# Packed weights, a 512-column output projection and stream keys by channel in a hybrid encoder step

## The chip, the cores and the metric

The kernel runs on one core of one Trainium2 chip. The metric is the device time of one launch, in microseconds. Work on the host before and after the launch (laying out inputs, reshaping outputs) is outside of it.

## What is computed

One layer of a streaming encoder, for 1024 prompt tokens and 8 streams of 16 new tokens, each stream with 512 past keys. All data is fp32.

```
h = RMSNorm(x) * g_pre;  z = h @ w_in                 # 2048 -> 7760 columns: q k v ga qi ki wi bg cg hc gb
iscore = sum_h relu(qi_h . ki) * wi_h                 # 16 index heads of 64 channels
sel = top_k(iscore, 256)  (132 for a stream)          # keys of later 64-frame chunks excluded
attn = softmax(q . k[sel]) @ v[sel]                   # 8 heads, 2 key/value heads, 128 channels
conv = bg * conv3(cg * hc)                            # causal, depthwise
y = x + RMSNorm(concat(attn*silu(ga), conv*silu(gb)) @ w_out) * g_post
```

Also returned: the new k, v and ki of every token, and the last two rows of cg*hc.

## The kernel before

Activations lie transposed on chip (`act_hi`, `act_lo`: 128 channels by 16 channel blocks by tokens). Each fp32 product is made as three fp32r products: high times high, high times low, low times high. ScalarE rounds a weight block to `w_hi` (`split_high`, line 1085), GpSimd makes the rest `w_lo` (line 813), VectorE makes the low parts of other operands (`low`, line 1338).

The work is a list of 154 tiles, each cut into 8 slots. Group A is 512 prompt tokens and the 128 stream tokens, group B the other 512 prompt tokens. Tiles 0 to 60 are the input projection of A (`gemm`, line 884: 96 matmuls a tile, 320 columns each), 61 to 121 that of B (48 of 512 columns), 122 to 137 the output projection of A, 138 to 153 that of B (`out_gemm`, line 914). There the stationary operand is a 128-token block of activations and the moving one 256 columns of `w_out`: 8 column groups ("pairs" of tiles), 5 token blocks in A and 4 in B. When a pair of tiles is done, VectorE multiplies all of its blocks by g_post (`product_out`, line 1475) and ScalarE sums their squares (`product_squares`, line 1176); the next pair goes on in the banks that are free. A's products go through `o_stage` to memory (`z_og`), B's stay in `o_nat`.

A planner (`timetable`) puts the attention's steps into slots by widths (`W`) that stand for their time. Every engine walks the same slots: the projection's part first, then the slot's steps. Each engine is a queue in order, SyncE (SP) too, which issues all DMAs. So a step waits for what lies ahead of it on its own engine. The steps that matter here:

- QS, IKS, HS, SEL (tiles 32 to 38, index scores of the streams). QS loads the index queries of all streams. IKS(b) loads 512 past index keys of stream b by token, transposes them on TensorE (4 transposes) and copies them. HS(b, 0 or 1) are two plain fp32 matmuls of 8 heads by 264 keys each (line 967), relu and weighting; SEL sums over heads (line 976).
- S, NRM, PT, ZZ (softmax of the prompt): scores (line 933), exponent (1235), normalising (1553), transposes (841), `pt_hi`/`pt_lo`, value product (984), gate (1594). Those of A and of the streams lie in tiles 62 to 76, those of B in tiles 109 to 131.
- KS, SS, PS, VS (softmax of the streams). KS(b) loads past keys by token, transposes them (8 transposes) and copies them to `kts`.
- RMS and FIN: the last norm and the residual sum (line 1633), 5 blocks of A beside the output projection of B, 4 blocks of B after its end.

`turn` (tiles kiwi, k, v) transposes new keys and values back to rows for the outputs. A weight half-tile of 512 KB comes by one DMA in rows of 512 bytes (1 KB for `w_out`), three buffers deep.

## Time and profile before

| | |
|---|---|
| runs | 2347.27, 2348.95, 2344.57 us; median 2347.27 |
| profiled execution | 2350.01 us; span from first to last instruction 2348.2 us |
| TensorE matmul busy | 2264.2 us, 96% of the span; granted clock 0.99 on average |
| VectorE / ScalarE / GpSimd busy | 992.8 (42%) / 718.2 (31%) / 757.9 us (32%) |
| chain that ended last | TensorE 84%, of it line 884 57% and line 914 16% of the span; VectorE 9% |
| DMA | 276.85 MB in 404152 packets, 382753 of them under 2 KB |

The busy share of TensorE is a union of instructions whose ends are modelled. To see what a matmul costs, take a run of matmuls with nothing between them from the chain of waits and divide its length by their number. Where the chain leaves TensorE, TensorE was waiting for the piece named.

### The profile page before, as it was taken

How to read it: one execution, taken by the hardware profiler on the slowest of the kernel's cores; microseconds unless marked ns; L12 is line 12 of the kernel's file. 1: busy time of each engine (PE TensorE's matmuls, PEld its weight loads, DVE VectorE, ACT ScalarE, POOL GpSimd, SP SyncE). 2: the span in 40 equal slices, each digit the busy share in tenths (PEclk: the TensorE clock that was granted, in tenths of full speed). 3: DMA queues.
4: the chain of work that ended last, by engine and by line, in shares of the span. 5: the costliest groups of instructions: out<-in, count | busy, mean ns of one | idle time of the engine just before them, and what ended most of it. 6: DMA issues, size and time to landing. Idle time of an engine off the chain costs nothing.

```text
span 2348.2 us, 33612 instructions
## 1 busy us (share of the span) xinstructions
PE 2264.2 (96%) x13997; PEld 2084.1 (89%) x13997; DVE 992.8 (42%) x1702; ACT 718.2 (31%) x1089; POOL 757.9 (32%) x328
## 2 busy tenths in 40 slices
PE   5999999999999999999998999999999999999996
PEld 5999998999999999877777888887877899999996
DVE  4000006891161112355213969797885634303212
ACT  5121123312211124343333242424223633324221
POOL 4333332232233333322222434342432222233442
PEclk9999999999999999999999999999999999999998
DMA  4433342343223244454654433334342524137644
GB/s 163 118 91 104 104 110 64 88 89 84 67 78 87 78 124 137 115 149 129 174 152 123 128 104 103 98 103 110 87 123 81 192 79 126 52 108 236 244 146 169
DMA packets 404152, 276.85 MB, mean 118 GB/s; under 512 B 36065, under 2 KB 382753, under 8 KB 401953
## 3 DMA queue, kind: packets, MB, share of 16 engines
q1 hardware_dynamic: 404000, 274.71, 40.1%
q8 instruction: 111, 1.82, 0.3%
q14 instruction: 41, 0.33, 0.0%
HBM read 230.58 MB, written 44.09 MB: 117 GB/s over the span
## 4 chain that ended last, share of the span: by engine, by line
PE 84%; DVE 9%; issue 2%; ACT 2%; DMA 2%; SPq 1%; DVEq 0%; ACTq 0%
PE ps L884 57%; PE ps L914 16%; PE ps L933 4%; PE ps L841 2%; PE ps L984 2%; DVE isc L1515 2%; DVE top L1514 1%; PE ps L1056 1%; DVE act_lo L1338 1%; DVE isc L1502 1%; DVE F L1553 1%; PE ps L967 1%; DMA conv<-z_mix 1%; DVE F L1577 1%; DMA w_raw<-in_w_in 0%
## 5 line engine op out<-in xcount | busy, mean ns | idle before, releaser
L813 POOL TENSOR_TENSOR w_lo<-w_raw,w_hi 128x1024 fp32r<-128x1024 f32 x308 | 743.2, 2413 | 1538.0 <-ACT w_hi L1085 1537.9
L884 PE MATMUL ps<-act_hi,w_hi 128*128 128x320 f32 (+1 forms) x2928 | 839.9, 340 | 6.8 <-DVE act_lo L1338 4.1
L884 PE MATMUL ps<-act_hi,w_lo 128*128 128x320 f32 (+1 forms) x2928 | 831.2, 337 | 0.0
L884 PE MATMUL ps<-act_lo,w_hi 128*128 128x320 f32 (+1 forms) x2928 | 831.0, 337 | 0.0
L884 PEld LDWEIGHTS ps<-act_hi,w_hi 128*128 128x128 f32 x2928 | 512.4, 189 | 54.0 <-issue 14.2
L1085 ACT ACTIVATE w_hi<-w_raw 128x1024 fp32r<-128x1024 f32 x308 | 326.1, 1059 | 753.4 <-PE ps L884 533.1
L884 PEld LDWEIGHTS ps<-act_hi,w_lo 128*128 128x128 f32 x2928 | 512.0, 188 | 39.6
L884 PEld LDWEIGHTS ps<-act_lo,w_hi 128*128 128x128 f32 x2928 | 512.7, 189 | 35.4
L914 PE MATMUL ps<-w_hi,act_hi 128*128 128x256 f32 x1152 | 326.9, 284 | 1.6 <-ACTq L1152 1.0
L914 PE MATMUL ps<-w_hi,act_lo 128*128 128x256 f32 x1152 | 326.1, 283 | 0.0
L914 PE MATMUL ps<-w_lo,act_hi 128*128 128x256 f32 x1152 | 326.0, 283 | 0.0
L914 PEld LDWEIGHTS ps<-w_hi,act_hi 128*128 128x128 f32 x1152 | 220.8, 192 | 4.2 <-ACTq L1152 1.2
L914 PEld LDWEIGHTS ps<-w_lo,act_hi 128*128 128x128 f32 x1152 | 220.9, 192 | 1.9
L914 PEld LDWEIGHTS ps<-w_hi,act_lo 128*128 128x128 f32 x1152 | 221.0, 192 | 0.0
L1514 DVE MAX8 top<-isc 128x8 f32<-128x384 f32 (+6 forms) x209 | 183.9, 880 | 9.9 <-DVE cs_p L1404 0.5
L1515 DVE MATCH_REPLACE8 isc<-top,isc 128x384 f32<-128x384 f32 (+6 forms) x209 | 180.0, 861 | 0.0
L1502 DVE SCALAR_TENSOR_TENSOR isc<-ps,wi_nat,isc 128x384 f32<-128x384 f32 (+5 forms) x90 | 85.6, 951 | 59.6 <-ACT ps L1199 54.5
L841 PE MATMUL ps<-ident,F 128*128 128x128 f32 (+2 forms) x504 | 76.8, 284 | 26.9 <-DVE F L1365 11.9
L1338 DVE TENSOR_TENSOR pt_lo<-ps,pt_hi 128x512 fp32r<-128x512 f32 x72 | 49.5, 690 | 121.0 <-ACT pt_hi L1085 121.0
L1148 ACT ACTIVATE ev<-ps 128x640 f32<-128x640 f32 (+1 forms) x58 | 37.6, 648 | 203.7 <-PE ps L884 203.7
L1199 ACT ACTIVATE ps<-ps 128x384 f32<-128x384 f32 (+5 forms) x96 | 68.0, 740 | 98.6 <-PE ps L933 98.6
L1526 DVE MEMSET msk<- 128x64 uint32 (+1 forms) x2 | 0.3, 138 | 228.9 <-DMA z_mask<-msk 228.6
(147 smaller groups left out, 1522.8 us busy)
## 6 DMA issues: line engine op xcount, KB each, us to landing
w_raw<-in_w_in SPq DMA_DIRECT2D x244, 512.0 KB, 4.0
w_raw<-in_w_out SPq DMA_DIRECT2D x64, 512.0 KB, 4.2
qraw<-z_qi SPq DMA_DIRECT2D x24, 256.0 KB, 4.8
fin_x<-in_x_prompt SPq DMA_DIRECT2D x6, 1024.0 KB, 8.3
conv<-z_mix SPq DMA_DIRECT2D x16, 320.0 KB, 4.0
z_og<-ev SPq DMA_DIRECT2D x8, 640.0 KB, 4.5
fin_o<-z_og SPq DMA_DIRECT2D x5, 1024.0 KB, 5.4
out<-fin_o SPq DMA_DIRECT2D x10, 512.0 KB, 5.0
```

Source lines behind the costliest of these rows:

```text
L813: nc.gpsimd.tensor_tensor(w_lo[:, r], w_raw[:, r], w_hi[:, r].bitcast(F32), ALU.subtract).then_inc(sem_w_lo, 1)
L841: return nc.tensor.transpose(out, in_, ident[0:in_.shape[0], 0:in_.shape[0]])
L884: last = nc.tensor.matmul(ps[:, bank + x, 0:w], wt[:, r, k % 8], a[:, k, w * x:w * (x + 1)], start=(k == 0 and wt is w_hi and a is act_hi) ...
L914: last = nc.tensor.matmul(out_place(pair, i), a[:, kk, z], out_weights(wt, h)[:, k], start=(kk == 0 and part == 0 and opens), stop=(kk == ...
L933: last = nc.tensor.matmul(ps[:, bank + x, 0:c], lhs, rhs[:, c * x:c * (x + 1)], start=(i == 0), stop=(i == len(operands) - 1))
L984: last = nc.tensor.matmul(ps[:, 4, :], lhs[:, P * j:P * j + P], rhs[:, p % 2], start=(j == 0 and i == 0), stop=(j == count - 1 and i == 2))
L1085: return nc.scalar.activation(out, in_, ACT.Copy)
L1199: nc.scalar.activation(v, v, ACT.Relu, scale=(ID * IH * 1.0) ** -0.5).then_inc(sem_relu, 1)
L1338: return nc.vector.tensor_tensor(out, x, hi.bitcast(F32), ALU.subtract)
L1502: ins = nc.vector.scalar_tensor_tensor(out=like(isc), in0=v, scalar=wi, in1=like(isc), op0=ALU.mult, op1=ALU.add)
L1514: link(nc.vector.max(top8[:], isc[:, 0:w]))
L1515: link(nc.vector.match_replace(isc[:, 0:w], top8[:], isc[:, 0:w], NEG_TAKEN))
```

## The change

The output projection takes 512 columns of `w_out` at a time: 4 column groups of 4 tiles. A has now 4 token blocks there, B has 5 (the stream block moved from A to B). Each block has a bank of its own and is multiplied, squared and, in A, stored by itself, one slot after its last matmul; A's stores go through three staging rows (`o_stage`). B uses eight banks. The activations of B are converted from tile 134 on, behind A's last column group. The softmax steps of B beside the output projection are placed 1.2 times as wide (`so`). FIN does 4 blocks beside B and 5 after it.

The host lays out `w_in` and `w_out` so that one DMA of a half-tile reads rows of 4 KB, and hands over `cache_k` and `cache_idx_k` by channel. The transposes of IKS and KS go away. New k and ki are outputs by channel, and k is not turned any more. KS has two buffers, and starts loading only when the last PT of A is done. The index queries of the streams are loaded twice, into partitions 0 to 63 and 64 to 127; ScalarE rounds all, VectorE makes the upper half the low part, and HS multiplies this stacked operand by the high and then by the low part of the keys (loaded twice too): four fp32r matmuls of 264 columns instead of two fp32 ones.

```diff
--- before.py
+++ after.py
...
-OUTP = [("o", i, 2 * P * (i // 2)) for i in range(KT)]
-OW, PAIRS = 2 * P, KT // 2
+OUTP = [("o", i, 4 * P * (i // 4)) for i in range(KT)]
+OW, PAIRS = 4 * P, KT // 4
+COLUMNS = [t[:2] for t in PROJ["A"]]
+OT = {"A": 4, "B": 5}
+OUT_COLUMN = {"A": 0, "B": 512}
+OUT_TOKENS = {"A": 512, "B": T_ALL - 512}
+SHARE = {"A": ((0,), (1,), (2,), (3,)), "B": ((0, 1), (2,), (3,), (4,))}
...
-TURNED = ("kiwi", "k", "v")
+TURNED = ("kiwi", "v")
...
+Z_B = SLOTS * (OUT_B - 4) + 4
 def z_pieces(slot):
 
     n, s = divmod(slot, SLOTS)
     if n == PHASE_LAST[1]:
         return [(0, 2 * s), (0, 2 * s + 1)]
-    if n == PHASE_LAST[2]:
-        return [(1, 2 * s), (1, 2 * s + 1)] if s < 4 else [(1, 4 + s)]
-    return [(1, 12 + s)] if n == PHASE_LAST[2] + 1 and s < 4 else []
+    c, late = divmod(slot - Z_B, 4)
+    return [(1, 2 * c), (1, 2 * c + 1)] if 0 <= c < KT // 2 and not late else []
+def z_loads(slot):
+    n, s = divmod(slot, SLOTS)
+    if n == PHASE_LAST[1]:
+        return [(0, k) for k in range(KT) if s == max(0, (k - 4) // 2)]
+    c, late = divmod(slot + 7 - Z_B, 4)
+    return [(1, 2 * c), (1, 2 * c + 1)] if 0 <= c < KT // 2 and not late else []
+def ended(slot):
+    n, s = divmod(slot - 1, SLOTS)
+    if not 0 <= n < NT or TILES[n][1] != "o" or TILES[n][2] % 4 != 3 or s < 4:
+        return []
+    return [(n, i) for i in SHARE[TILES[n][0]][s - 4]]
...
-    place([(step, 2) for step in second] + softmax_b[cut:], 2 * NP + 1.7, OUT_B - 1)
-    place([(("RMS", "A"), 3)] + [(("FIN", i), 16) for i in range(5)], OUT_B + 1, OUT_B + 14)
-    side[TAIL] = [("RMS", "B")] + [("FIN", i) for i in range(5, 9)]
+    place([(step, 2) for step in second] + wider(softmax_b[cut:], W["so"]), 2 * NP + 1.7, OUT_B - 1)
+    place([(("RMS", "A"), 3)] + [(("FIN", i), 16) for i in range(4)], OUT_B + 1, OUT_B + 14)
+    side[TAIL] = [("RMS", "B")] + [("FIN", i) for i in range(4, 9)]
...
-    if kind in ("KS", "QI") and n > 0:
+    if kind == "QI" and n > 0:
         return same[n - 1]
+    if kind == "KS":
+        return [s for s in ORDER if s[0] == "SS"][n - 2] if n > 1 else [s for s in before_it if s[0] == "PT"][-1]
...
+        o_stage = [ev[:, 0, 0:OW], ev[:, 1, 0:OW], conv[:, 2560:3072]]
...
+        qs_raw = F[:, 0:2048].rearrange("p (b h q) -> p b h q", b=NB, h=IH)
+        qs_v = qv[:].rearrange("p (b h q) -> p b h q", b=NB, h=IH)
+        ik_raw = F[:, 2048:2048 + 2 * KEYS_S].rearrange("p (u x) -> p u x", u=2)
+        r_s = F[:, 3104:3104 + KEYS_S]
+        ik_hi = [keys_hi[:, 0:KEYS_S], q_hi[:].rearrange("p u t -> p (u t)")[:, 0:KEYS_S]]
+        ik_lo = [keys_lo[:, 0:KEYS_S], q_lo[:].rearrange("p u t -> p (u t)")[:, 0:KEYS_S]]
+        kts = F[:, 0:4 * KEYS_S].rearrange("p (u k x) -> p u k x", u=2, k=2)
...
+            return 4 * pair + i if pair < PAIRS else 4 * PAIRS + 5 * (pair - PAIRS) + i
 
         def out_place(pair, i):
-            return ps[:, bank_use(pair, i) % 4, OW * (i % 2):OW * (i % 2 + 1)]
+            use = bank_use(pair, i)
+            return ps[:, use % 4 if pair < PAIRS else (use - 4 * PAIRS) % 8, 0:OW]
...
+                    _, kind, index, _ = TILES[h // 2]
+                    src = w_in[COLUMNS.index((kind, index)), h % 2] if kind != "o" else \
+                        w_out[index // 4, 2 * (index % 4) + h % 2]
+                    sp.dma_start(w_raw[:, h % RING].rearrange("p k e -> p (k e)"), src
+                                 ).then_inc(sem_w_ld[h % RING], 16)
...
+            def store_product(n, i):
+                c, use = TILES[n][3], bank_use(TILES[n][2] // 4, i)
+                sp.wait_ge(sem_o_cp, use + 1)
+                sp.dma_start(z_og[P * i:P * (i + 1), c:c + OW], o_stage[use % 3]).then_inc(sem_og_out[use % 3], 16)
...
+                    for r in range(2):
+                        for b in range(NB):
+                            c = 512 + NS * b
+                            sp.dma_start(qs_raw[ID * r:ID * r + ID, b], z_qi[:, c:c + NS].rearrange("(h d) q -> d h q", d=ID)
+                                         ).then_inc(sem_qs_ld, 16)
...
-                    sp.dma_start(ik_new, z_kiwi[0:ID, 512:T_A]).then_inc(sem_qs_ld, 16)
+                                         ).then_inc(sem_wi_ld, 16)
                 elif kind == "IKS":
                     b = step[1]
+                    spilled("A", "kiwi", 0)
                     sp.wait_ge(sem_x_read, 5)
-                    sp.wait_ge(sem_iks_tr, max(b - 1, 0))
-                    sp.dma_start(iknat[:, b % 2], cache_idx_k[0, b].rearrange("(t p) d -> p t d", p=P)
-                                 ).then_inc(sem_iks_ld[b % 2], 16)
+                    sp.wait_ge(sem_iks_lo, max(b - 1, 0))
+                    for r in range(2):
+                        part = ik_raw[ID * r:ID * r + ID, b % 2]
+                        sp.dma_start(part[:, 0:PAST], cache_idx_k[b]).then_inc(sem_iks_ld[b % 2], 16)
+                        sp.dma_start(part[:, PAST:KEYS_S], z_kiwi[0:ID, 512 + NS * b:512 + NS * (b + 1)]
+                                     ).then_inc(sem_iks_ld[b % 2], 16)
...
-                    sp.wait_ge(sem_ks_tr, b)
-                    sp.dma_start(knat, cache_k[0, b].rearrange("(t p) k d -> p t (k d)", p=P)
+                    sp.wait_ge(sem_pt_pe, PT_A)
+                    sp.wait_ge(sem_ss_pe, max(b - 1, 0))
+                    sp.dma_start(kts[:, b % 2, :, 0:PAST], cache_k[b]).then_inc(sem_ksk_ld[b % 2], 16)
+                    c = 512 + NS * b
+                    sp.dma_start(kts[:, b % 2, :, PAST:KEYS_S], z_k[:, c:c + NS].rearrange("(k d) t -> d k t", d=P)
                                  ).then_inc(sem_ksk_ld[b % 2], 16)
...
+                pair, c, h = index // 4 + PAIRS * (group == "B"), 2 * (index % 4) + s // 4, 2 * n + s // 4
                 if s % 4 == 0:
                     pe.wait_ge(sem_w_lo, h + 1)
-                units = [(k, i) for j in range(0, tiles, 2) for k in range(4) for i in range(j, min(j + 2, tiles))]
-                for x, (k, i) in enumerate(units[tiles * (s % 4):tiles * (s % 4 + 1)]):
-                    kk = 4 * quarter + k
+                for i in SHARE[group][s % 4]:
                     use = bank_use(pair, i)
-                    if kk == 0 and i % 2 == 0:
+                    if c == 0:
                         if use < 4:
                             pe.wait_ge(sem_evac[use // 2], NP)
-                        pe.wait_ge(sem_nat_sq, max(use - 3, 0))
-                    if pair % PAIRS == 0 and i == 0:
-                        pe.wait_ge(sem_z_lo, kk + 1 + KT * (group == "B"))
-                    z = slice(P * i, P * (i + 1))
-
-                    opens, closes = i % 2 == 0, i % 2 == 1 or i == tiles - 1
-                    for part, (a, wt) in enumerate(((act_hi, w_hi), (act_hi, w_lo), (act_lo, w_hi))):
-                        last = nc.tensor.matmul(out_place(pair, i), a[:, kk, z], out_weights(wt, h)[:, k],
-                                                start=(kk == 0 and part == 0 and opens),
-                                                stop=(kk == KT - 1 and part == 2 and closes))
+                        elif pair < PAIRS:
+                            pe.wait_ge(sem_nat_sq, use - 3)
+                        else:
+                            pe.wait_ge(sem_nat_sq, max(use - 7, 4 * PAIRS))
+                            if use == 4 * PAIRS + 4:
+                                pe.wait_ge(sem_z_dve, UNITS)
+                    for k in range(2):
+                        kk, z = 2 * c + k, slice(P * i, P * (i + 1))
+                        if pair % PAIRS == 0 and i == 0:
+                            pe.wait_ge(sem_z_lo, kk + 1 + KT * (group == "B"))
+                        for part, (a, wt) in enumerate(((act_hi, w_hi), (act_hi, w_lo), (act_lo, w_hi))):
+                            last = nc.tensor.matmul(out_place(pair, i), a[:, kk, z], out_weights(wt, h)[:, k],
+                                                    start=(kk == 0 and part == 0), stop=(kk == KT - 1 and part == 2))
+                    if c == KT // 2 - 1 and i < OT[group] - 1:
+                        last.then_inc(sem_o_pe, 1)
...
-                elif kind == "IKS":
-                    b = step[1]
-                    pe.wait_ge(sem_iks_ld[b % 2], 16 * (b // 2 + 1))
-                    pe.wait_ge(sem_isum, HEADS_A)
-                    pe.wait_ge(sem_hs_r, 2 * b)
-                    for t in range(4):
-                        last = transpose(ps[0:ID, 4, P * t:P * t + P], iknat[:, b % 2, t])
-                    last.then_inc(sem_iks_tr, 1)
                 elif kind == "HS":
                     _, b, j = step
-                    pe.wait_ge(sem_iks_cp, b + 1)
-                    pe.wait_ge(sem_qs_ld, 16 * 25)
+                    pe.wait_ge(sem_iks_lo, b + 1)
+                    pe.wait_ge(sem_qs_lo, 1)
+                    pe.wait_ge(sem_isum, HEADS_A)
                     pe.wait_ge(sem_hs_r, n)
+                    lhs = qs_v[:, b, 8 * j:8 * j + 8].rearrange("p h q -> p (h q)")
                     for x in range(2):
-                        lhs = qs_v[:, b, 8 * j:8 * j + 8].rearrange("p h q -> p (h q)")
-                        last = nc.tensor.matmul(ps[:, 4 + x, 0:HALF_S], lhs, ikt[:, HALF_S * x:HALF_S * (x + 1)],
-                                                start=True, stop=True)
+                        cut = slice(HALF_S * x, HALF_S * (x + 1))
+                        for i, rhs in enumerate((ik_hi[b % 2], ik_lo[b % 2])):
+                            last = nc.tensor.matmul(ps[:, 4 + x, 0:HALF_S], lhs, rhs[:, cut], start=(i == 0), stop=(i == 1))
                     last.then_inc(sem_hs_pe, 1)
...
-                    pe.wait_ge(sem_ksk_ld[b % 2], 16 * (b // 2 + 1))
-                    pe.wait_ge(sem_z_dve, UNITS_A)
-                    pe.wait_ge(sem_ps_cp, max(b - 1, 0))
-                    for kv in range(2):
-                        for t in range(4):
-                            last = transpose(ps[:, 4 + kv, P * t:P * t + P], knat[:, t, P * kv:P * kv + P])
-                    last.then_inc(sem_ks_tr, 1)
                 elif kind == "SS":
                     b = step[1]
-                    pe.wait_ge(sem_ks_cp, b + 1)
-                    pe.wait_ge(sem_qqs_ld, 16 * (NB + 2))
+                    pe.wait_ge(sem_ksk_ld[b % 2], 32 * (b // 2 + 1))
+                    pe.wait_ge(sem_qqs_ld, 16 * (NB + 1))
+                    pe.wait_ge(sem_z_dve, UNITS_A)
...
+            def product_squares(n, i):
 
                 group, _, index, _ = TILES[n]
+                pair = index // 4 + PAIRS * (group == "B")
+                use = bank_use(pair, i)
+                act.wait_ge(sem_nat_sq, max(use - 1, 0))
...
+                act.wait_ge(sem_o_cp, use + 1)
+                nc.scalar.activation(o_junk[use % 2], out_place(pair, i), ACT.Square,
+                                     accum_out=o_ssq[:, i, index // 4:index // 4 + 1]).then_inc(sem_nat_sq, 1)
...
+                elif kind == "QS":
+                    act.wait_ge(sem_qs_ld, 16 * 2 * NB)
+                    act.wait_ge(sem_head_pe, HEADS_A)
+                    copy(qv[:], F[:, 0:2048]).then_inc(sem_qs_hi, 1)
                 elif kind == "IKS":
                     b = step[1]
-                    act.wait_ge(sem_iks_tr, b + 1)
-                    act.wait_ge(sem_hs_pe, 2 * b)
-                    if b == 0:
-                        act.wait_ge(sem_qs_ld, 16 * 25)
-                    copy(ikt[:, PAST:KEYS_S], ik_new[:, NS * b:NS * (b + 1)])
-                    copy(ikt[:, 0:PAST], ps[0:ID, 4, :]).then_inc(sem_iks_cp, 1)
+                    act.wait_ge(sem_iks_ld[b % 2], 64 * (b // 2 + 1))
+                    act.wait_ge(sem_head_pe, HEADS_A)
+                    act.wait_ge(sem_hs_pe, 2 * max(b - 1, 0))
+                    copy(ik_hi[b % 2], ik_raw[:, b % 2]).then_inc(sem_iks_hi, 1)
...
+            def product_out(n, i):
 
                 group, _, index, c = TILES[n]
+                pair = index // 4 + PAIRS * (group == "B")
+                use = bank_use(pair, i)
+                if i == OT[group] - 1:
+                    dve.wait_ge(sem_gemm, 2 * n + 2)
+                else:
+                    dve.wait_ge(sem_o_pe, use - pair + 1)
...
                 if group == "A":
-                    dve.wait_ge(sem_og_out, 16 * pair)
-                if pair == PAIRS:
+                    dve.wait_ge(sem_og_out[use % 3], 16 * (use // 3))
+                if use == 4 * PAIRS:
                     dve.wait_ge(sem_z_out, 16 * UNITS)
+                out = o_stage[use % 3] if group == "A" else o_nat[:, i, c:c + OW]
+                nc.vector.tensor_tensor(out, out_place(pair, i), gbc[:, c:c + OW], ALU.mult).then_inc(sem_o_cp, 1)
...
+                elif kind == "QS":
+                    dve.wait_ge(sem_qs_hi, 1)
+                    low(qv[64:128, :], F[64:128, 0:2048], qv[64:128, :]).then_inc(sem_qs_lo, 1)
+                elif kind == "IKS":
+                    b = step[1]
+                    dve.wait_ge(sem_iks_hi, b + 1)
+                    low(ik_lo[b % 2], ik_raw[:, b % 2], ik_hi[b % 2]).then_inc(sem_iks_lo, 1)
...
+        if name == "w_in":
+            a = np.stack([a[0, :, col:col + P].reshape(2, 8, P, P).transpose(0, 2, 1, 3).reshape(2, P, 8 * P)
+                          for _, _, col in PROJ["A"]])
+        if name == "w_out":
+            a = a[0].reshape(8, 2, P, PAIRS, OW).transpose(3, 0, 2, 1, 4).reshape(PAIRS, 8, P, 2 * OW)
...
+        if name == "cache_k":
+            a = a[0].transpose(0, 3, 2, 1)
+        if name == "cache_idx_k":
+            a = a[0].transpose(0, 2, 1)
```

## Rows read from the trace of the kernel before

**Rows 1.** Page, section 1: busy us, share, instructions.
```profile
PE 2264.2 (96%) x13997; PEld 2084.1 (89%) x13997; DVE 992.8 (42%) x1702; ACT 718.2 (31%) x1089; POOL 757.9 (32%) x328
```

**Rows 2.** Groups by line and shape, TensorE: count, busy us, mean ns, idle before.
```profile
L884 PE MATMUL ps<-act_hi,w_hi 128*128 128x512 f32 x976 | 386.9, 396 | 2.4 <-DVEq L1428 1.5 <-DVEq L1406 0.6 <-PE ps L841 0.3
L914 PE MATMUL ps<-w_hi,act_hi 128*128 128x256 f32 x1152 | 326.9, 284 | 1.6 <-ACTq L1152 1.0 <-ACT nat L1176 0.4
```

**Rows 3.** Chain of waits, whole span: start us, us, what.
```profile
120.56 246.40 PE ps L884 x1680
...
549.47 3.72 PE ps L884 x24
554.27 3.72 PE ps L884 x24
...
1509.09 91.13 PE ps L884 x402
...
2055.77 75.61 PE ps L914 x630
```

**Rows 4.** The 64 records of line 967 (HS): duration ns, first and last start.
```profile
L967 PE MATMUL ps<-F x64: 382/383/488, 533.9 to 645.9; 64*128 64x264 f32 x64
```

**Rows 5.** Chain, 0 to 75 us: one `turn` of five transposes.
```profile
61.50 0.55 PE ps L841 x5
```

**Rows 6.** Chain, 543 to 552 us: one IKS.
```profile
544.43 0.44 PE ps L841 x4
```

**Rows 7.** Chain, 1153 to 1172 us: one KS.
```profile
1157.28 0.87 PE ps L841 x8
```

**Rows 8.** Timeline, end: VectorE, then SP's DMA issues: start us, us.
```profile
2330.59 1.42 DVE L1475 TENSOR_TENSOR o_nat<-ps,gbc 128x256 f32<-128x256 f32 x4 [21.62 <-PE ps L914]
...
2334.74 4.88 DVE L1633 SCALAR_TENSOR_TENSOR o_nat<-o_nat,stat,fin_x 128x1024 f32<-128x1024 f32 x4
...
2336.06 8.70 SPq L725 DMA_DIRECT2D out<-o_nat  x8
```

**Rows 9.** Groups by line and shape, VectorE and ScalarE.
```profile
L1594 DVE TENSOR_TENSOR zat<-ps,sga 128x512 f32<-128x512 f32 x16 | 11.0, 690 | 23.1 <-PE ps L984 23.1
L1085 ACT ACTIVATE pt_hi<-ps 128x512 fp32r<-128x512 f32 x72 | 43.0, 597 | 115.5 <-PE ps L841 115.5
L1577 DVE CUSTOM_DVE_ANT_0 F<-ps,msk 128x1024 f32<-128x1024 f32 x8 | 9.7, 1218 | 8.0 <-PE ps L933 8.0
L1235 ACT ACTIVATE F<-F,stat 128x1024 f32<-128x1024 f32 x8 | 9.2, 1151 | 17.2 <-DVE stat L1581 17.2
L1338 DVE TENSOR_TENSOR qv<-qraw,qv 64x1024 fp32r<-64x1024 f32 x12 | 23.5, 1961 | 17.0 <-ACT qv L1085 16.3
L1338 DVE TENSOR_TENSOR q_lo<-qraw,q_hi 128x512 fp32r<-128x512 f32 x16 | 16.9, 1054 | 3.5 <-ACT q_hi L1085 3.3
L1085 ACT ACTIVATE qv<-qraw 128x1024 fp32r<-128x1024 f32 x12 | 12.6, 1048 | 0.0
```

**Rows 10.** TensorE timeline, 2147.5 to 2149.6 us: first matmul that waited in B.
```profile
2148.85 0.39 PE L914 MATMUL ps<-w_hi,act_hi 128*128 128x256 f32 x1 [0.22 <-ACT nat L1176]
```

**Rows 11.** Stretch of A's output projection with softmax: busy of each engine, clock, DMA.
```profile
1853.00:2059.00 206.00, 204.08 (x1548) 196.81 (x1547) 82.47 (x168) 79.51 (x149) 47.90 (x20) 1.00 0.32 99
```

**Rows 12.** VectorE timeline at tile 32, its last work before HS.
```profile
528.08 0.82 DVE L1427 TENSOR_TENSOR conv<-ps,conv 128x640 f32<-128x640 f32 x1
```

**Rows 13.** SP timeline, the loads of QS and the weight load behind them.
```profile
490.12 7.49 SPq L613 DMA_DIRECT2D F<-z_qi  x8
...
507.43 0.59 SPq L520 DMA_DIRECT2D w_raw<-in_w_in  x1
```

**Rows 14.** DMA issues: count, KB each, median us from issue to landing.
```profile
w_raw<-in_w_in SPq DMA_DIRECT2D x244, 512.0 KB, 4.0
...
out<-o_nat SPq DMA_DIRECT2D x8, 512.0 KB, 3.0
F<-z_qi SPq DMA_DIRECT2D x8, 64.0 KB, 3.6
```

221 lines of the change are left out of this document (89 added, 132 removed).

## Prediction

> **What bounds the kernel now.** First the page: TensorE is busy 2264.2 of 2348.2 us and no other engine half of that [rows 1]; the reader sees that only TensorE can set the time. Then the runs of matmuls in the chain of waits, for the busy time does not say what a matmul costs [rows 3]: 246.40 us / 1680 = 146.7 ns for 320 columns, 91.13 / 402 = 226.7 ns for 512, 75.61 / 630 = 120.0 ns for 256. The three lie on one line: 192 columns more cost 80.0 ns, so 2.4 columns a nanosecond (the upper of the clock's two levels; the stretch of rows 11 shows a granted clock of 1.00) and 13.3 ns that each matmul costs whatever its width. The 154 tiles at these prices are some 1938 us; the rest of the span is attention work on TensorE and waits. So what counts is how many TensorE instructions go, and where TensorE would wait anew.
>
> **The change part by part.**
>
> Output projection. Before, 3 x 1152 = 3456 matmuls of 256 columns [rows 2] at 120.0 ns: 414.9 us (rounded to the 120.1 of all of them: 415.1). After: 4 column groups x 9 token blocks x 16 channel blocks x 3 = 1728 of 512 columns at 226.7: 391.7. Term: -23.3 us. The columns are the same; what goes is 1728 times the fixed 13.3. The Trainium skill, "TensorE: Matmul & The Clock Gate", section "Back-to-back issue gap", gives N / 2.4 + 2.5 ns for a warm matmul; by that the term would be only 1728 x 2.5 = 4.3 us. The rows show 13.3 at all three widths, in a stream where each matmul has a weight load of its own, so the measurement decides.
>
> HS in fp32r. From one run of 24 matmuls to the next it is 554.27 - 549.47 = 4.80 us with one HS between; 24 x 0.1467 = 3.52, so one HS costs TensorE 1.28 us [rows 3]. It is four records of 264 columns (64 in 16 steps) [rows 4]. After: four fp32r matmuls at 264 / 2.4 + 13.3 = 123.3 ns, 0.49 us. 16 x 0.79 = -12.6 us. Bounds: if a part of the 1.28 is lost at the border between kinds and stays, 0.4 of it does, +6; if nothing else, 0.
>
> Transposes that go: IKS 8 x 0.44 = 3.5 us [rows 6]; KS 8 x 0.87 = 7.0 us [rows 7]; k tiles, two of A at 0.55 [rows 5] and two of B with four transposes, 0.44 [rows 6], 2.0 us. Together -12.5. They lie between projection matmuls on the engine that bounds, so all of it counts. ScalarE's copies of them and VectorE's copies of k go too; these engines have room [rows 11], so that is worth nothing by itself. KS's place in the plan stays.
>
> End. B has 5 blocks behind its last matmul instead of 4. The eight stores of four blocks follow each other at (8.70 - 0.33) / 7 = 1.20 us, the pace of the final sums (4.88 / 4) [rows 8]; two more are +2.4. Before them one product of 512 columns (0.69) and one square (0.60 and the reading of the sum, some 0.2) [rows 9] take the place of four products (1.42) [rows 8] and squares up to 2.4 us: -0.7. Term +1.7, bounds +1 and +3.5 (the stores' DMA, 3.0 us each [rows 14], may set the pace).
>
> Border from A to B. B's first matmul asks for all 16 squares of A, and the 16th belongs to the block that ended just before it. TensorE waits for the last matmul's latency beyond its turn (0.39 - 0.23), product 0.69, square 0.60 + 0.2, hand-overs 0.1: 1.8 us; before it waited 0.22 once in B [rows 10]. Term +1.6, bounds +1 and +2.5. In exchange B's first activations are converted long before.
>
> Waits in A's output projection. A bank is wanted again three slots after its last matmul: 3 x 6 x 0.2267 = 4.1 us, and softmax work of the slots besides. Product and square need 1.6, so 2.5 are spare. Ahead of the product on VectorE may stand one score step of 1024 keys (mask and maximum 1.22, small ones, the division of the head before, about 2.6 together), ahead of the square one exponent, 1.15 [rows 9]: at worst 2.6 + 1.4 - 2.5 = 1.5 us each, for the 8 reuses (two ends of column groups) that lie beside softmax: 12 us. At best the 206.00 - 204.08 = 1.9 us of idle TensorE in this stretch before [rows 11] go too. Softmax itself has slots that are shorter (1.36 for 1.80 us), but 1.2 times as many, and VectorE is busy 82 of 206 us. I take 3 us, +1.1 net, nearest to the row, bounds -2 and +12. The three staging rows: a store of 256 KB must land within about three slots; one of 512 KB takes 3.0 [rows 14], so it is hidden. If SP comes late with it, that is in the same 12.
>
> QS and IKS. VectorE is at work until 528.9 [rows 12], then lows of 2 x 1.96 and 1.05 [rows 9]: 533.9. ScalarE's copy of the queries (2 x 1.05) lies beside VectorE's older work. The first HS was at 533.9 before [rows 4], and 0.4 us of IKS ahead of it are gone: +0.6, bounds 0 and +4. SP holds up the queue behind QS for 507.43 - 490.12 = 17.3 us; eight more loads at 7.49 / 8 make it 24.3 [rows 13]. The weight load behind them is then 7 us later; it feeds tile 32's second half, wanted at about 528, and needs 4.0 [rows 14] and two roundings (some 3.5): ready at about 522. Hidden, with 6 us to spare.
>
> KS loads start behind the last PT now, six slots (8.2 us and more) before SS(0); one of 512 KB takes 4 us: hidden. SP must wait there and issues 20 DMAs behind it, at 0.45 us each 9 us, about four slots with their softmax work; by the plan the weight load behind them is wanted eight slots later.
>
> Packed weights. No wait of the projections' matmuls is put down to a weight load [rows 2]. The load may land in 3.0 instead of 4.0 us, as the stores with 4 KB rows do [rows 14]. Three stand among the input loads before the first matmul: -0.5, bounds +0.5 and -3.
>
> Sum: -23.3 - 12.6 - 12.5 + 1.7 + 1.6 + 1.1 + 0.6 - 0.5 = -43.9 us. The profiled execution took 2350.0 (span 2348.2 and 1.8 around it), so 2306.1; the median of the runs is 2.7 below the profiled one: 2303.4, I say 2303.
>
> **The rivals.**
>
> Drains hold TensorE (12 us and more instead of 1.1 in A). For: all is in order on VectorE and ScalarE, and a bank has one owner. Against: VectorE is 60% idle there. 2303 + 11 = 2314, up to 2320.
>
> Halving the number buys nothing: the 13.3 ns goes with 256 columns and not with an instruction, 240 ns for 512. Then the first term is 0 and the time 2326. Against: line 884 shows 226.7 at 512 columns. The skill's 2.5 ns (same page and section) would come close to this in its result, at 2322.
>
> HS keeps its border cost, since SEL stays plain fp32: 2309.
>
> The other side: SP chokes on QS. 16 loads of 64-byte pieces instead of 8 fill the queues; if each blocks SP until the one before has landed (3.6 us [rows 14]), they take 58 us instead of 7.5. Beyond 13 us more than before (7 to reach the slack above, 6 of slack), the weights come late and TensorE stands: at 3.6 us a load 50 - 13 = 37 us of standing, 2340; under their own crowd, at 5 us a load, 80 - 7.5 - 13 = 59 us, 2362, slower than before. It decides from about 4.0 us a load on. Against: the eight took 0.94 each.
>
> That the change does not do what it says: the counts of matmuls would show it; I see nothing for it.
>
> **How the numbers follow.** Forecast (2296 to 2311) 0.76; drains 0.09 (2311 to 2320); HS border 0.06 (about 2309); 240 ns for 512 columns 0.03; SP 0.02, most of it beyond 2347; anything else 0.03, a quarter of it not faster. The skill's 2.5 ns has 0.01 besides. Range 2292 to 2320: below, every wait at its best bound and the opening's 3 us with some of the softmax waits of tiles 109 to 121 falling away; above, the drains' bound. About 0.2% of the time is what a measurement of this kernel can tell from none, 4.7 us: faster 0.97, same 0.01, slower 0.02.
>
> **What would show it.** Chain: runs of 512-column matmuls in the output projection at 226.7 ns each. TensorE records at the new HS line 64 of 264 columns, 0.5 us a step. About 114 transposes fewer. The output projection from its first matmul to the last some 457 us where it was 477. TensorE waits of about 1.8 us once, at the first matmul of B, and together under 5 us in A. Ten final sums, 1.2 us apart. Packets down from 404152 to 130 to 150 thousand, and nothing on TensorE moving by it. The prediction is wrong if matmuls of 512 columns cost over 230 ns, if TensorE waits more than 8 us in A's output projection, or if tiles 29 to 33 show a wait for weights.

## The result, and the profile after

| | before | after |
|---|---|---|
| runs, us | 2347.27, 2348.95, 2344.57, 2345.94 | 2312.73, 2311.65, 2310.35, 2317.49 |
| median | 2346.61 | 2312.19 |
| profiled execution (span) | 2350.01 (2348.2) | 2312.73 (2310.9) |

The ratio is 0.9857, 95% interval 0.9838 to 0.9876: 34.4 us faster, where 43.9 were forecast (about 2303 us). Between the two profiled executions the difference is 37.3 us, and these two are what the tables below take apart.

Page of the kernel after, section 1 (busy us, share, instructions), and the line of packets:

```profile
PE 2220.0 (96%) x12155; PEld 1978.3 (86%) x12155; DVE 1013.0 (44%) x1667; ACT 707.2 (31%) x994; POOL 759.8 (33%) x328
...
DMA packets 160680, 274.65 MB, mean 119 GB/s; under 512 B 42656, under 2 KB 94880, under 8 KB 158624
```

TensorE is still the only engine that can set the time, with 1842 instructions fewer than in [rows 1]: 1728 in the output projection and 114 transposes. Groups by line and shape of the kernel after, to set against [rows 2] and [rows 4] (count, busy us, mean ns, idle before):

```profile
L947 PE MATMUL ps<-w_hi,act_hi 128*128 128x512 f32 x576 | 227.0, 394 | 9.2 <-issue 4.7 <-ACTq L1173 4.5
L996 PE MATMUL ps<-q_hi,qv 128*128 128x264 f32 x16 | 4.2, 282 | 0.0
```

The first line says more than its count: 9.2 us of idle TensorE in two pieces, where [rows 2] had 1.6 in all. The chain of waits of the kernel after gives the price of a wide matmul, its timeline an HS step (start us, us, what):

```profile
2084.89 206.73 PE ps L947 x912
```
```profile
543.05 0.29 PE L996 MATMUL ps<-q_hi,qv 128*128 128x264 f32 x1
543.17 0.29 PE L996 MATMUL ps<-q_lo,qv 128*128 128x264 f32 x1
543.30 0.28 PE L996 MATMUL ps<-q_hi,qv 128*128 128x264 f32 x1
543.42 0.28 PE L996 MATMUL ps<-q_lo,qv 128*128 128x264 f32 x1
543.53 0.46 PE L916 MATMUL ps<-act_hi,w_hi 128*128 128x320 f32 x2
```

206.73 / 912 = 226.7 ns, as [rows 3] had it for the projections; an HS step is 543.53 - 543.05 = 0.48 us.

Where the 37.3 us between the two profiled executions come from, by the starts of the projection matmuls that open the tiles:

| stretch | before | after | difference |
|---|---|---|---|
| to the start of tile 32 | 521.0 | 517.3 | -3.7 |
| tiles 32 to 39, stream index | 143.8 | 128.5 | -15.3 |
| tiles 40 to 70 | 463.3 | 463.8 | +0.5 |
| tiles 71 to 76, key loads and KS | 113.2 | 107.1 | -6.1 |
| tiles 77 to 89 | 174.2 | 169.1 | -5.1 |
| tiles 90 to 121 | 437.8 | 437.0 | -0.8 |
| output projection, first matmul to last | 476.9 | 468.4 | -8.5 |
| behind the last matmul's start | 17.9 | 19.7 | +1.8 |

The forecast for the output projection was 457. Its matmuls did get shorter by 23.2 us (3456 at 120.1 against 1728 at 226.7 ns), but 14.7 us of waits and slow matmuls came in. Two places hold 12.2 us of them; the rest is spread.

**The entry (tile 122).** TensorE, then ScalarE of the kernel after; below them the granted clock of TensorE (the number behind the parenthesis) by stretch:

```profile
1831.61 0.80 PE L947 MATMUL ps<-w_hi,act_hi 128*128 128x512 f32 x1 [4.48 <-ACTq L1173]
```
```profile
1827.32 1.15 ACT L1259 ACTIVATE F<-F,stat 128x1024 f32<-128x1024 f32 x1 [2.09 <-DVE stat L1608]
...
1828.47 1.13 ACT L1106 ACTIVATE act_hi<-conv 128x512 fp32r<-128x512 f32 x2
...
1829.62 1.28 ACT L1169 ACT_TABLE_LOAD   x1
...
1830.91 0.60 ACT L1169 ACTIVATE ev<-ps 128x512 f32<-128x512 f32 x1
```
```profile
1822.00:1831.60 9.60, 5.12 (x23) 0.97 0.51 159
1831.60:1838.00 6.40, 6.39 (x22) 0.77 0.92 287
```

The third block of the first column group opens bank 2, which still holds tile 121. ScalarE empties it (1830.91) behind an exponent, two pieces of A's gated output and a table load. TensorE waits 4.65 us. Before, a bank held two half-width blocks, the same bank was wanted two blocks later, and TensorE waited 1.16 us:

```profile
1863.07 0.39 PE L914 MATMUL ps<-w_hi,act_hi 128*128 128x256 f32 x1 [1.00 <-ACTq L1152]
```

Behind the wait of the kernel after, 7 matmuls ran wholly or in part at the lower level of the clock and cost 1.45 us more; the 0.77 of the second stretch says the same (0.23 of 6.40 us).

**The border from A to B (tile 138).** TensorE; then GpSimd, VectorE and ScalarE in order of time; then the clock:

```profile
2070.98 0.76 PE L947 MATMUL ps<-w_hi,act_hi 128*128 128x512 f32 x1 [4.70 <-issue]
2071.54 0.63 PE L947 MATMUL ps<-w_lo,act_hi 128*128 128x512 f32 x1
```
```profile
2062.08 2.40 POOL L845 TENSOR_TENSOR w_lo<-w_raw,w_hi 128x1024 fp32r<-128x1024 f32 x1 [2.09 <-ACT w_hi L1106]
...
2062.66 3.24 DVE L1353 TENSOR_TENSOR act_lo<-conv,act_hi 128x640 fp32r<-128x640 f32 x2 [1.25 <-ACT act_hi L1106]
2065.82 1.28 DVE L1496 TENSOR_TENSOR ev<-ps,gbc 128x512 f32<-128x512 f32 x2
2067.01 0.68 DVE L1496 TENSOR_TENSOR conv<-ps,gbc 128x512 f32<-128x512 f32 x1
2069.41 0.69 DVE L1496 TENSOR_TENSOR ev<-ps,gbc 128x512 f32<-128x512 f32 x1 [1.72 <-DMA z_og<-ev]
...
2070.19 0.60 ACT L1197 ACTIVATE nat<-ps 128x512 bf16<-128x512 f32 x1 [0.78 <-DVE ev L1496]
```
```profile
2071.00:2077.00 6.00, 6.00 (x15) 0.51 0.87 274
```

B's first matmul waits for A's last square (2070.19), that for the last product (2069.41), and that stands 1.72 us for its staging row. The row is late because the products before it were: VectorE was busy with low parts of B's pieces, 3.24 us for a pair of operations that take 0.81 us each when GpSimd is still. After 4.87 us of wait come 14 matmuls with a step of about 0.43 instead of 0.227 us, at a granted clock of 0.51: the lower level, 1.2 GHz. That is 2.8 us more.

### The profile page after: what moved, and what is told of

Read it like the earlier page. It is cut to its first block, busy times and chain, and to the rows that moved or that the text cites. A ratio compares the mean times of both kernels' runs of the same rounds, so it can differ in the third digit from the quotient of the medians.

```text
span 2310.9 us, 29863 instructions
## 1 busy us (share of the span) xinstructions
PE 2220.0 (96%) x12155; PEld 1978.3 (86%) x12155; DVE 1013.0 (44%) x1667; ACT 707.2 (31%) x994; POOL 759.8 (33%) x328
## 2 busy tenths in 40 slices
DMA packets 160680, 274.65 MB, mean 119 GB/s; under 512 B 42656, under 2 KB 94880, under 8 KB 158624
## 3 DMA queue, kind: packets, MB, share of 16 engines
q1 hardware_dynamic: 160544, 272.74, 35.5%
## 4 chain that ended last, share of the span: by engine, by line
PE 83%; DVE 11%; issue 2%; ACT 2%; DMA 1%; DVEq 0%; SPq 0%; ACTq 0%
PE ps L916 57%; PE ps L947 17%; PE ps L967 4%; DVE isc L1534 2%; DVE top L1533 2%; PE ps L1012 2%; PE ps L873 2%; DVE isc L1521 1%; PE ps L1077 1%; DVE F L1580 1%; DVE act_lo L1353 1%; DVE F L1604 0%; DVE conv L1436 0%; DVE o_nat L1660 0%; DMA F<-in_x_prompt 0%
## 5 line engine op out<-in xcount | busy, mean ns | idle before, releaser
L947 PE MATMUL ps<-w_hi,act_hi 128*128 128x512 f32 x576 | 227.0, 394 | 9.2 <-issue 4.7
L947 PE MATMUL ps<-w_lo,act_hi 128*128 128x512 f32 x576 | 226.1, 393 | 0.0
L947 PE MATMUL ps<-w_hi,act_lo 128*128 128x512 f32 x576 | 225.9, 392 | 0.0
L947 PEld LDWEIGHTS ps<-w_hi,act_hi 128*128 128x128 f32 x576 | 109.1, 189 | 32.5 <-issue 5.1
L947 PEld LDWEIGHTS ps<-w_hi,act_lo 128*128 128x128 f32 x576 | 109.1, 189 | 23.5
L947 PEld LDWEIGHTS ps<-w_lo,act_hi 128*128 128x128 f32 x576 | 109.1, 189 | 22.6
L873 PE MATMUL ps<-ident,F 128*128 128x128 f32 (+1 forms) x408 | 63.7, 287 | 27.0 <-DVE F L1380 14.6
```

Source lines behind the costliest of these rows:

```text
L873: return nc.tensor.transpose(out, in_, ident[0:in_.shape[0], 0:in_.shape[0]])
L947: last = nc.tensor.matmul(out_place(pair, i), a[:, kk, z], out_weights(wt, h)[:, k], start=(kk == 0 and part == 0), stop=(kk == KT - 1 and ...
```

## The experiments

Medians are in us; the ratio is to the kernel before, measured beside each (its medians: 2346.61 for after, 2347.26 for e1 to e4, 2347.25 for e5 to e8, 2344.70 for e9 to e12). "Entry" and "border" are from the profiled execution alone. They give TensorE's wait and, behind the +, what the slow matmuls right after it cost: the time from start to start less (columns / 2.4 + 13.4) ns, summed until the steps are normal again. Where e6 and e8 have a second wait, the cost behind it is read from the granted clock, since several kinds of matmul follow there.

| kernel | median | ratio, 95% | entry | border |
|---|---|---|---|---|
| after | 2312.19 | 0.9857 (0.9838 to 0.9876) | 4.65 + 1.45 | 4.87 + 2.83 |
| e1 split | 2333.06 | 0.9942 (0.9926 to 0.9958) | 4.45 + 2.48 | 4.53 + 1.43 |
| e2 hs32 | 2324.73 | 0.9908 (0.9894 to 0.9922) | 4.34 + 1.57 | 4.84 + 2.89 |
| e3 unpack | 2313.53 | 0.9858 (0.9844 to 0.9872) | 4.61 + 2.12 | 4.76 + 1.63 |
| e4 stage4 | 2311.59 | 0.9857 (0.9840 to 0.9873) | 4.50 + 2.36 | 3.98 + 1.67 |
| e5 zlate | 2308.76 | 0.9839 (0.9819 to 0.9859) | 4.55 + 2.28 | 2.40 + 0.08 |
| e6 astart | 2313.41 | 0.9860 (0.9838 to 0.9882) | 2.35, then 3.91 + 1.7 | 4.86 + 1.65 |
| e7 zshift | 2312.91 | 0.9856 (0.9837 to 0.9875) | 4.60 + 1.43 | 4.18 + 1.53 |
| e8 best | 2308.06 | 0.9844 (0.9822 to 0.9866) | 2.37, then 3.93 + 1.7 | 3.09 + 0.08 |
| e9 again | 2311.57 | 0.9872 (0.9850 to 0.9893) | 4.52 + 2.36 | 4.88 + 1.68 |
| e10 zlate, stage4 | 2311.89 | 0.9863 (0.9846 to 0.9880) | 4.81 + 2.83 | 2.01 + 0.08 |
| e11 one piece | 2307.77 | 0.9845 (0.9830 to 0.9859) | 3.56 + 2.81 | 2.15 + 0.08 |
| e12 rows64 | 2322.76, one run | | 4.57 + 2.26 | 4.87 + 1.66 |

**e1, the width alone.**

```diff
-last = nc.tensor.matmul(out_place(pair, i), a[:, kk, z], out_weights(wt, h)[:, k], ...)
+for y in range(2):
+    half = slice(OW // 2 * y, OW // 2 * (y + 1))
+    last = nc.tensor.matmul(out_place(pair, i)[:, half], a[:, kk, z], out_weights(wt, h)[:, k, half], ...)
```

> Undoes the width alone: each 512-column multiplication of the output projection is two of 256 columns with the same stationary block, 3456 where the changed kernel has 1728. Theory A (the halving is worth what the two kernels' rows say, 2 x 120.1 - 226.7 = 13.5 ns a pair): +23.3 us over the changed kernel, some 2335 us, less what of the 15.5 us of TensorE's waits in A's output projection (tiles 122 to 137) vanishes because the products come later, 0 to 3 us. Rival B (a second multiplication with the stationary block that stands already costs only its columns, about 106.7 ns): no more than 2 us over the changed kernel.

0.9942 against 0.9857 is +20 us; the output projection went from 468.4 to 488.3, +19.9. Chain of e1, and one of its three groups of weight loads:

```profile
2084.93 222.97 PE ps L949 x1858
```
```profile
L949 PEld LDWEIGHTS ps<-w_hi,act_hi 128*128 128x128 f32 x1152 | 183.7, 193 | 13.1 <-ACTq L1177 4.7
```

222.97 / 1858 = 120.0 ns: the 13.3 ns goes with each matmul. Theory A holds and rival B's time is refuted. Its mechanism was not tested, though: the trace has 3456 weight loads, so the second matmul of a pair loads the same stationary block once more, and what it would cost without that load is not shown. 3.4 us of the 23.3 did not come; 1.7 of them lie at the border, where the clock was low for a shorter time (14 steps of 0.2 us here, 14 of 0.43 in the kernel after). Executions of one kernel differ in that too (e9 has 1.68 there for 2.83), so it need not be an effect of the width. The larger finding is the other difference: with the old width, the new order of the output projection takes 11.4 us more than the old one (488.3 against 476.9).

**e2, the fp32 head scores.** Two plain fp32 matmuls over 64 rows in place of four in fp32r over the stacked 128.

```diff
-for i, rhs in enumerate((ik_hi[b % 2], ik_lo[b % 2])):
-    last = nc.tensor.matmul(ps[:, 4 + x, 0:HALF_S], lhs, rhs[:, cut], start=(i == 0), stop=(i == 1))
+last = nc.tensor.matmul(ps[:, 4 + x, 0:HALF_S], lhs, ik_raw[0:ID, b % 2, cut], start=True, stop=True)
```

> Undoes the stacked index scores alone: each step of the head scores is again two plain fp32 multiplications of 264 columns, with keys and queries by channel as loaded. Theory A (the term of the prediction, 16 x (1.28 - 0.49) us): +12.6 us over the changed kernel, some 2325 us. Rival B (part of those 1.28 us was the cost of entering fp32, which the head selection's multiplications, still fp32, now pay: 3 x 0.10 + 0.19 us, 8 times, some 4 us in all): +8.5 to +9.5 us, some 2321 us, and the selection's records in this kernel are short again.

0.9908 against 0.9857: +12.0 us by the runs; tiles 32 to 39 take 141.1 where they took 128.5, +12.6. Theory A to the tenth. Timeline of e2, a selection step and a score step:

```profile
542.34 1.05 PE L1006 MATMUL ps<-F,sel 128*128 128x264 f32 x4
543.04 0.65 PE L919 MATMUL ps<-act_hi,w_hi 128*128 128x320 f32 x2
```
```profile
546.84 1.15 PE L998 MATMUL ps<-F 64*128 64x264 f32 x4
547.92 0.56 PE L919 MATMUL ps<-act_hi,w_hi 128*128 128x320 f32 x2
```

Both steps are four records of plain fp32 with 264 columns, 0.222 us from one start to the next inside. The selection, over 128 rows, leaves TensorE after 0.70 us, and the matmul behind it takes the rest of 4 x 0.222. The scores, over 64 rows, leave it after 1.08, and the matmuls on both sides are longer too: together 1.28, which is 0.39 more than 4 x 0.222. So what I had called the border of fp32 is not one of precision. e12 asks whether it is one of rows.

**e12, 64 rows in fp32r.** Only rows 0 to 63 are multiplied; the kernel leaves out the low part of the queries.

```diff
-lhs = qs_v[:, b, 8 * j:8 * j + 8].rearrange("p h q -> p (h q)")
+lhs = qs_v[0:ID, b, 8 * j:8 * j + 8].rearrange("p h q -> p (h q)")
...
-last = nc.tensor.matmul(ps[:, 4 + x, 0:HALF_S], lhs, rhs[:, cut], start=(i == 0), stop=(i == 1))
+last = nc.tensor.matmul(ps[:, 4 + x, 0:HALF_S], lhs, rhs[0:ID, cut], start=(i == 0), stop=(i == 1))
```

> The head scores in fp32r as in the changed kernel, but over 64 rows only: the low parts of the queries are left out. The plain fp32 form over 64 rows cost 1.28 us a step, of it 0.39 us beyond 4 x 0.222 us, in the multiplications at its two ends (239 for 147 ns before, 327 for 222 and 313 for 222 ns inside, 252 for 147 ns behind). Theory A (the change between 128 and 64 rows costs it, at either precision): 0.49 + 0.3 to 0.4 us a step, 16 times, +5 to +6.5 us on the stream index. Rival B (only plain fp32 over 64 rows has it): 0.49 us a step, no difference.

Tiles 32 to 39 take 134.5 instead of 128.5: +6.0, 0.38 us a step. Timeline of e12:

```profile
544.81 0.46 PE L916 MATMUL ps<-act_hi,w_lo 128*128 128x320 f32 x2
545.20 0.39 PE L996 MATMUL ps<-q_hi,qv 64*128 64x264 f32 x1
545.42 0.28 PE L996 MATMUL ps<-q_lo,qv 64*128 64x264 f32 x1
545.54 0.28 PE L996 MATMUL ps<-q_hi,qv 64*128 64x264 f32 x1
545.66 0.28 PE L996 MATMUL ps<-q_lo,qv 64*128 64x264 f32 x1
545.87 0.56 PE L916 MATMUL ps<-act_hi,w_hi 128*128 128x320 f32 x2
```

The first score matmul takes 0.22 us to the next start where the kernel after had 0.12, the last 0.21, and each neighbour some 0.1 more. Theory A: the change from 128 rows to 64 and back costs 0.38 us a step in fp32r, 0.39 in plain fp32 (e2). So of the 12.6 us that HS brought, 6.0 came from the filled rows and 6.6 from fp32r. That is for this order of work, where a step stands between matmuls of 128 rows. The one total of e12 says little by itself: it is 11.2 us above the median of e9, of which 6.0 are in these tiles and some 4 in tiles 77 to 89, for the reason that e7 shows.

**e3, the packing.** Loads from the matrices as they come.

```diff
-src = w_in[COLUMNS.index((kind, index)), h % 2] if kind != "o" else w_out[index // 4, 2 * (index % 4) + h % 2]
+dst, src = w_raw[:, h % RING], w_in_v[:, KT // 2 * (h % 2):KT // 2 * (h % 2 + 1), col:col + P]
+if kind == "o": ...
```

> Undoes the packing alone: the weights are loaded from the matrices as they come, in rows of 512 bytes (input projections) and 2 KB (output projection). Theory A (transfers hidden behind TensorE, the term was -0.5 us): 0 to +1 us over the changed kernel, and no wait of TensorE for a weight. Rival B (smaller packets delay the stream's and the other loads by their share of the DMA engines): +1.5 to +4 us, with new waits at the tiles of the stream index or at the start.

0.9858 against 0.9857: nothing, though the packets are 387496 again instead of 160680 and the DMA engines' share 40.5% instead of 35.5%. No new wait on TensorE. The packing has no part in the result.

**e4, a fourth staging row.**

```diff
-o_stage = [ev[:, 0, 0:OW], ev[:, 1, 0:OW], conv[:, 2560:3072]]
+o_stage = [ev[:, 0, 0:OW], ev[:, 1, 0:OW], conv[:, 2560:3072], sb("o_row", [P, OW])[:]]
```

> A fourth staging row for A's sums in the output projection. In the changed kernel TensorE waits 4.87 us at the border from group A to group B; the fourth product there waits for a staging row until 1.72 us after its data. Theory A (row and queue order each have their part): the wait at the border falls by 1 to 1.8 us and the total by as much, 2310.5 to 2311.5 us. Rival B (the order on VectorE alone decides, low parts of B's gated output ahead of A's last products): no change, below 0.5 us, with the border wait above 4.4 us.

The border's wait fell from 4.87 to 3.98 us, and the product no longer waits for a row. The total moved by less than the runs can tell. By the trace that is nearer to A than to B, though below A's range; the row alone is not what holds the border.

**e5, B's last two pieces late.**

```diff
+if slot in (Z_B + 29, Z_B + 33):
+    c = 6 + (slot - Z_B - 29) // 4
+    return [(1, 2 * c), (1, 2 * c + 1)]
```

> The last two pieces (of eight) of group B's gated output are converted one and five slots into B's own output projection, so that VectorE has A's last products ahead of them. In the changed kernel TensorE waits 4.87 us at the border from A to B. Theory A (VectorE's queue order makes that wait): it falls by 2 to 4 us, to 1 to 3 us, of which up to 1.7 us may stay for the staging row; some 2309 us. Rival B (the staging row alone, or the evacuation of the last accumulation): above 4 us still, no change of the time.

VectorE now takes each product as its matmuls end, and the clock stays up:

```profile
2062.45 0.69 DVE L1499 TENSOR_TENSOR ev<-ps,gbc 128x512 f32<-128x512 f32 x1 [1.76 <-PE ps L950]
2063.81 0.69 DVE L1499 TENSOR_TENSOR ev<-ps,gbc 128x512 f32<-128x512 f32 x1 [0.67 <-PE ps L950]
2065.17 0.69 DVE L1499 TENSOR_TENSOR conv<-ps,gbc 128x512 f32<-128x512 f32 x1 [0.67 <-PE ps L950]
2067.16 0.69 DVE L1499 TENSOR_TENSOR ev<-ps,gbc 128x512 f32<-128x512 f32 x1 [1.29 <-DMA z_og<-ev]
```
```profile
2068.74 0.47 PE L950 MATMUL ps<-w_hi,act_hi 128*128 128x512 f32 x1 [2.24 <-issue]
2069.04 0.39 PE L950 MATMUL ps<-w_lo,act_hi 128*128 128x512 f32 x1
```
```profile
2068.70:2075.00 6.30, 6.26 (x28) 1.00 0.49 172
```

The wait is 2.40, and the slow matmuls are gone: 7.70 us at the border became 2.48. The output projection takes 463.9 instead of 468.4. Theory A: the wait gave 2.47 us, and the clock gave 2.75 besides (1.6 if e9 is taken for the kernel after). The median is 3.4 us lower, but the intervals of the ratios overlap, so the cause is shown by the traces and not by the totals.

**e6, A's last two pieces late.**

```diff
-        return [(0, 2 * s), (0, 2 * s + 1)]
+        return [(0, 2 * s), (0, 2 * s + 1)] if s < 6 else []
+    if n == PHASE_LAST[1] + 1 and s in (1, 3):
+        return [(0, 11 + s), (0, 12 + s)]
```

> The last two pieces of A's gated output are converted one and three slots into A's output projection, behind ScalarE's evacuation of the tile before. In the changed kernel TensorE waits 4.66 us at the entry (before: 1.16 us). Theory A (the third block needs the bank that ScalarE has still to evacuate, and the evacuation stands behind the conversions of the last pieces, the exponents and the table load): the wait falls by 2 to 4.6 us, to at most 2.5 us; some 2308.5 us. Rival B (the table load of 1.28 us and the evacuation's place behind the softmax alone set it): it stays above 4 us, or the wait only turns up again at the multiplications that want pieces 6 and 7.

```profile
1829.19 0.50 PE L949 MATMUL ps<-w_hi,act_hi 128*128 128x512 f32 x1 [2.18 <-ACTq L1175]
1840.10 0.66 PE L875 MATMUL ps<-ident,F 128*128 128x128 f32 x4 [3.75 <-DVE F L1582]
```

The place was right and the gain was not: the wait at the entry is 2.3 us shorter, and 3.9 us came in at 1840, where TensorE turns probabilities whose exponent and normalising had stood behind the moved conversions. The output projection takes 469.2 us. Nearest is rival B in its second half: the wait turns up again, though at the softmax and not at the multiplications that want pieces 6 and 7.

**e7, all of B's pieces two slots later.**

```diff
-Z_B = SLOTS * (OUT_B - 4) + 4
+Z_B = SLOTS * (OUT_B - 4) + 6
```

> Every conversion of B's gated output is two slots later, away from the slots in which GpSimd makes the low parts of the weights. Theory A (VectorE's operation with two inputs in SBUF stands while GpSimd's runs): the pairs of low parts take 1.6 us where they take up to 3.24 us, and the wait at the border falls by 1 to 2.5 us, unless the later start gives it back: between -2.5 and +1 us on the total. Rival B (the low parts are slow for another reason, their own data): the pairs stay at a mean of 2.4 us or more.

It did not part what it was to part: GpSimd's operations moved with the pieces (it starts one at 2057.24, VectorE's pair follows at 2057.82 and takes 3.24 us again). The wait fell to 4.18. Nothing is decided by it. Its trace has something else, though, which the kernel before shows as well. VectorE, GpSimd and TensorE of the kernel after, then of e7, ahead of the first multiplications with a prefetched key tile:

```profile
1233.50 1.22 DVE L1353 TENSOR_TENSOR qv<-qraw,qv 64x1024 fp32r<-64x1024 f32 x1
...
1234.47 2.50 POOL L845 TENSOR_TENSOR w_lo<-w_raw,w_hi 128x1024 fp32r<-128x1024 f32 x1 [2.08 <-ACT w_hi L1106]
...
1234.82 0.39 PE L967 MATMUL ps<-keys_hi,qv 128*128 128x320 f32 x1 [0.23 <-issue]
```
```profile
1236.51 2.34 POOL L845 TENSOR_TENSOR w_lo<-w_raw,w_hi 128x1024 fp32r<-128x1024 f32 x1 [1.05 <-ACT w_hi L1106]
1236.57 3.36 DVE L1353 TENSOR_TENSOR qv<-qraw,qv 64x1024 fp32r<-64x1024 f32 x1
...
1240.03 0.60 PE L967 MATMUL ps<-keys_hi,qv 128*128 128x320 f32 x1 [3.40 <-issue]
```

In e7 GpSimd starts 0.06 us ahead, VectorE's operation takes 3.36 for 1.22 us, and TensorE is idle for 3.4 us and goes on at the lower clock. The kernel before had the same:

```profile
1262.60 0.61 PE L933 MATMUL ps<-keys_hi,qv 128*128 128x320 f32 x1 [3.40 <-issue]
```

Which of the two starts first differs from execution to execution like the toss of a coin, and it is worth 4 us. All 14 traces bear it out. In five (before, e7, e8, e10, e12) GpSimd started 0.06 to 0.34 us ahead and VectorE's operation took 3.25 to 3.36 us; in the other nine VectorE was ahead, by as little as 0.03 us in e9, and took 1.22. Tiles 77 to 89 took 169.0 to 170.5 us in the kernel after, e1 to e6, e9 and e11, and 173.1 to 173.5 in e7, e8, e10 and e12.

**e8, e4 to e6 in one.** The three edits above together.

> Three edits in one: the fourth staging row, B's last two pieces late, A's last two pieces late. Theory A (the shortfall against the forecast is the queue order at the two borders): the waits at both borders, 9.5 us together, fall to 1.5 to 3.5 us and the total by 6 to 8 us, to 2304 to 2306 us, below both kernels. Rival B (the waits move to later slots of the same tiles): the total falls by less than 3 us and the sum of waits in tiles 122 to 138 stays above 13 us.

Entry and border show what their parts had shown, and the second wait behind the entry eats what the entry gave. The output projection takes 465.8 us, where e5 alone has 463.9, and the medians of the two cannot be told apart. Theory A fails for the entry. Rival B describes it better: waits and the slow matmuls behind them come to 13.2 us in tiles 122 to 138, where the kernel after has 15.7, and by the ratios the total fell by 3 us. At the border the wait is 3.09, more than in e5, since now a weight is late:

```profile
2076.31 1.06 ACT L1111 ACTIVATE w_hi<-w_raw 128x1024 fp32r<-128x1024 f32 x1 [1.04 <-DMA w_raw<-in_w_out]
2077.28 0.58 ACT L1202 ACTIVATE nat<-ps 128x512 bf16<-128x512 f32 x1
```

ScalarE waits for a weight to land and does A's last square behind it.

**e9, the changed kernel again; e10, the edit of e5 with the staging row of e4.**

> The changed kernel once more, beside the next two. Two executions of one program differ in a coin: VectorE's low part of a query piece (1.22 us) ahead of key stream's multiplications near 1234 us starts before GpSimd's operation or stands behind it (3.36 us), and TensorE then has 0.4 or 3.56 us of wait. Theory A (that coin, the clock behind it and the first tile make the spread of one kernel's executions): median 2309 to 2316 us, and the profiled execution shows the one or the other. Rival B (the spread lies in the output projection): the waits at 1831 and 2071 us differ from 4.66 and 4.87 us by more than 1 us.

> The fourth staging row and B's last two pieces late, nothing else; the entry into A's output projection is left as it is. With the late pieces alone the wait at the border was 2.40 us and TensorE kept its full clock behind it, where the changed kernel had 14 multiplications of 0.43 us. Theory A (the row makes 1.29 us of the last product's 2.40 us): border 1.3 to 1.8 us, total 5 to 6.5 us below the changed kernel, about 2306 us. Rival B (a weight that lands late, in front of the last square on ScalarE, sets it once the row is free): border 2.4 to 3.2 us, no gain over the late pieces alone.

e9: theory A; in its profiled execution VectorE was ahead (169.9 us for tiles 77 to 89). The two waits stand where they stood (4.52 and 4.88), so they belong to the kernel and not to one execution. The slow matmuls behind them vary (1.5 or 2.4 us at the entry, 2.8 or 1.7 at the border). e10: a wait of 2.01, between the theories, and 0.4 us below e5 for the row. The last product ended at 2075.16 and its square began at 2075.51, behind the rounding of a weight on ScalarE, so with the row free that queue adds some 0.3 us. Its median does not show the gain; in its profiled execution GpSimd was ahead (3.4 us of idle at 1240.63). By my numbers this version should have won, and the runs do not say so.

**e11, and only A's last piece late.** This is e10 with the last piece of A, (0, 14) and (0, 15), converted in slot 1 of tile 122.

> As the one before, and of A's pieces only the last is moved, one slot into the output projection. With two moved the wait at the entry fell from 4.66 to 2.35 us and 3.91 us came in its place at 1840 us, since the conversions put off the exponents. Theory A (ScalarE's queue there has no room: what is moved comes back as a late softmax step): entry 3.3 to 3.7 us, a new wait of 1.5 to 3.9 us behind it, sum not below the 5 us of the changed kernel. Rival B (one piece fits between two exponents): entry 3.3 to 3.7 us, nothing behind it, 1 us gained.

The wait at the entry is 3.56 and nothing comes in its place, as rival B had it. The slow matmuls behind it cost 2.81 us, so wait and clock together are 6.4, against 6.9 in e9 and 7.6 in e10, its base. Its four runs, 2306.9 to 2308.3, all lie below the four of e9, 2310.5 to 2319.0. It has the lowest median here, 3.8 us below the changed kernel measured beside it; but the intervals of the two ratios overlap, and by ratio e5 (0.9839) and e8 (0.9844) are level with it (0.9845). Between the profiled executions of e9 and e11 the output projection gives 4.9 us; tiles 90 to 121, which no edit touches, vary as well (432.5 to 437.1 us over the thirteen executions), with waits of the same length and more or less time at the lower clock.

## Why the prediction was right, and what it missed

**The time.** 2312 us lies inside the range of 2292 to 2320, but outside the band of 2296 to 2311 that had 0.76; it is in the band that I had given to the drains, with 0.09. The terms that take time away came true one by one. What the two ends of the output projection add was put at 1.6 us and came to 12.2, and the range held because it had room for waits in the middle that did not come. That part is luck.

**Right, with its size.**

- 512 columns at 226.7 ns: the term was -23.3 us, the matmuls are shorter by 23.2, and e1 has +19.9.
- HS at 0.48 us a step: the term was -12.6, and e2 has +12.6 in the tiles that hold it.
- Transposes: 114 fewer. Tiles 71 to 76 are 6.1 us shorter, of the 7.0 for KS; in the later runs with the same steps they are 2.9 to 6.7 us shorter, less where the clock was low there for a while. The stream index is 15.3 us shorter, against 12.6 + 3.5 less the 0.6 for QS. No run undoes this part alone.
- The end: ten final sums at 1.2 us each, +1.8 where +1.7 was forecast.
- Packed weights: -0.5 forecast, 0 in e3.
- QS: SP was held 13.68 and 8.80 us by its loads, and no tile waited for a weight.
- Packets came to 160680, where 130 to 150 thousand were said; nothing hung on it.

**The step that failed: the border from A to B.** I added latency, product and square, 1.8 us, with the sentence that in exchange B's first activations are converted long before. The first are, but the low parts of the later pieces stand on VectorE in front of A's last products. The forecast's 1.8 us (term +1.6, bounds +1 and +2.5) measured 7.7: 4.87 of wait and 2.83 of slow matmuls (4.88 and 1.68 in e9). e5 shows the cause, by moving two pieces. What is left there, 2.4, falls to 2.0 with a fourth row (e10), near the forecast's 1.8. How much of the wait is due to GpSimd, which makes a pair of low parts take 3.24 us instead of 1.6, stays open; e7 was to tell and did not. A price for the clock behind a wait stood nowhere in the forecast.

**The step that was not there: the entry.** For banks I counted reuse within A's output projection and not the first use, where a bank has tile 121 in it. It cost 4.65 + 1.45 against 1.16 before, 4.9 us. e6 and e11 show the place, since the wait falls with what is moved out of ScalarE's queue. They show as well how little room there is beside the softmax: two pieces moved come back as another wait, one piece gives 1 us. To free the bank by another engine than ScalarE was not tried.

**Waits within A.** The forecast had 3 us, a term of +1.1; apart from the two ends there are 0.3 at 1883, 1.1 at 1889 and 0.5 at 1957, together 1.9. This held. Between the ends no bank was waited for, so the rival that drains hold TensorE did not come true there. At the two ends, though, what holds TensorE is the emptying of a bank and the last square, each behind other work on ScalarE or VectorE: that rival was right in kind and wrong in the place. With the entry A's output projection has 6.6 us of waits: over the 5 us that I had named, under the 8 us that would have refuted me; with the border it is 11.5.

**The rivals.** 240 ns for 512 columns: refuted by the chain. HS keeps its border cost since SEL is plain fp32: refuted by e2 (SEL pays none) and e12 (the cost was of 64 rows). SP chokes: 22.5 us for 32 loads and no weight late. The rule that the Trainium skill gives in "TensorE: Matmul & The Clock Gate", section "Back-to-back issue gap", N / 2.4 + 2.5 ns, which that section calls the gap of an isolated matmul, would have made the width worth 4.3 us. e1 has 20 us, so the measurement decides.

**The account.** The forecast's waits of the output projection were 2.7 us and came to 14.7: 12.0 short, 12.1 with the rounding of the matmuls. Outside it 5.5 us more fell away than forecast. Some 4 of them are the coin of tiles 77 to 89, which the profiled execution of the kernel before had against it. 1 more lies in the same tiles and 2 ahead of tile 32, whose start varies by 4 us between executions (516.0 to 520.2 in the later kernels); other stretches take some of it back. So 43.9 - 12.1 + 5.5 = 37.3 is for these two executions. By medians 34.4 stands against 43.9 - 12.1 = 31.8, and 2.6 are left that I cannot assign; the interval of the ratio is 4.5 us wide on each side.

## What to carry to other kernels

Cost the two ends of a changed loop with the same care as its inside. For the first use of each buffer and for the last drain, list everything that stands in front on the queue of the engine that frees it, the next phase's early work above all. Where an engine that bounds the time would stand for some microseconds, count the clock as well as the wait, and try first whether a piece of early work can go a few slots behind the border. Undo each part of a change by itself: here the width brought 20 us and the stacked scores 12, the packing nothing, and the new order cost 11 (from one execution of each kernel); the transposes' 10 or so were read from the trace alone.

## What the runs showed of the hardware

- A wait costs TensorE twice. At the border waits of 3.98 us and more were followed by 7 to 14 matmuls at half the clock (1.4 to 2.9 us), waits of 2.0 to 3.1 us by none. At the entry waits of 3.6 to 4.8 us were followed by 1.4 to 2.8 us, waits of 2.4 us by none. The same wait had different costs in different executions.
- Going from matmuls over 128 rows to ones over 64 and back costs 0.38 us a time in fp32r and 0.39 in plain fp32 (e12, e2).
- VectorE with two operands in SBUF stands while GpSimd works, if GpSimd started first: 3.36 for 1.22 us on the same instruction. With one operand in PSUM it doesn't: of 72 `pt_lo` operations of the kernel after, 51 clear of GpSimd took 688 ns on average and 19 wholly within one of its operations 691. The Trainium skill, "SBUF — State Buffer", section "SBUF: two separate sides", has this as an exclusive lock on a port pair that holds for the whole instruction and goes to the one that starts first. The traces agree: GpSimd was 0.06 us ahead in e7 and VectorE took 3.36 us; VectorE was 0.03 us ahead in e9 and took 1.22.
